# Diffusion trunk layer on one core: modulation in channel halves, q and kv in inner halves, scatter in pairs, latent tiles first

## The reference, cut to what matters

```
shift1, scale1, gate1, shift2, scale2, gate2 = split(silu(cond) @ w_ada + b_ada)
h    = x * (1 + scale1) + shift1
proj = h @ w_in        # columns: q 512 | kv 256 | k_rope 64 | hyena 3 x 1024 | gates 2 x 2048
q    = rms_norm(q_c) @ w_uq ;  kv = rms_norm(kv_c) @ w_ukv ;  attention, 8 heads
hy   = hyena(proj)     # short and long convolution
mix  = (sigmoid(g_a) * (attn @ w_o_mla) + sigmoid(g_b) * (hy @ w_o_hy)) @ w_out
x    = layer_norm(ALPHA * x + gate1 * mix)
h    = x * (1 + scale2) + shift2
aff  = softmax(h @ w_router)           # 16 experts
gate, idx = top_k(aff.T, cap)          # 16 of 128 context, 32 of 256 latent tokens an expert
ffn  = scatter_add(down(silu(gate_proj) * up_proj) * gate)
x    = layer_norm(ALPHA * x + gate2 * ffn)
```

## Time and profile before

| | us |
|---|---|
| median of 3 runs | 2348.67 (2346.88 to 2348.97) |
| profiled execution | 2348.09, span 2346.3 |
| TensorE matmul busy | 2150.9 (92%) |
| VectorE busy | 794.7 (34%) |
| ScalarE, GpSimd busy | 124.0, 54.0 |
| loads and stores | 667.79 MB, mean 285 GB/s |

### The profile page before, as it was taken

The page is one execution under the profiler, slowest core; times in us unless marked ns, Lnnn a source line. Parts: engine busy times, 40 slices in busy tenths (PEclk is TensorE's granted clock), DMA queues, the critical chain, the costliest instruction groups (busy, mean ns, idle before and its releaser), DMA issues.

```text
span 2346.3 us, 18784 instructions
## 1 busy us (share of the span) xinstructions
PE 2150.9 (92%) x8278; PEld 1069.6 (46%) x8278; DVE 794.7 (34%) x1095; ACT 124.0 (5%) x256; POOL 54.0 (2%) x99
## 2 busy tenths in 40 slices
PE   4698999999999999999999699999999999988884
PEld 1274455556555555555444363333333333332321
DVE  2201365546466658540023411112111211111116
ACT  0102310000000000000000100000000000000000
POOL 1100000000000001000100000000000000000000
PEclk9898999999999999999999899999999999999996
DMA  9943046531036666673599569999999999999992
GB/s 397 382 144 111 0 142 227 194 123 54 36 108 251 251 235 231 251 234 125 200 393 331 206 244 428 428 428 427 427 428 427 428 428 428 427 427 428 427 428 99
DMA packets 156272, 667.79 MB, mean 285 GB/s; under 512 B 9503, under 2 KB 89459, under 8 KB 116896
## 3 DMA queue, kind: packets, MB, share of 16 engines
q1 hardware_dynamic: 150544, 644.37, 69.3%
q0 software_dynamic: 5232, 19.09, 2.1%
q10 hardware_dynamic: 416, 3.15, 0.3%
HBM read 663.20 MB, written 3.38 MB: 284 GB/s over the span
## 4 chain that ended last, share of the span: by engine, by line
PE 73%; DMA 17%; DVE 9%; ACT 0%; issue 0%; ACTq 0%; DVEq 0%
PE ps L709 14%; DMA ring<-in_w_up_dram 14%; PE ps L900 10%; PE ps L866 8%; PE ps L740 7%; PE ps L1017 7%; PE ps L724 7%; DVE arena L1666 5%; PE ps L612 3%; DMA ring<-in_w_ada_dram 2%; PE ps L954 2%; PE ps L810 1%; PE ps L811 1%; PE ps L993 1%; PE ps L812 1%; PE ps L963 1%
## 5 line engine op out<-in xcount | busy, mean ns | idle before, releaser
L866 PE MATMUL ps<-ring,arena 128*64 128x512 f32 (+1 forms) x2048 | 456.3, 597 | 56.8 <-DMA ring<-in_w_up_dram 51.5
L709 PE MATMUL ps<-arena,ring 128*128 128x384 f32 x1024 | 331.9, 486 | 0.0
L866 PEld LDWEIGHTS ps<-ring,arena 128*64 128x64 f32 (+1 forms) x2048 | 142.1, 137 | 365.9 <-issue 258.9
L1239 DVE SCALAR_TENSOR_TENSOR arena<-ring,arena 128x2048 f32<-128x2048 f32 x120 | 282.2, 2352 | 54.9 <-DMA ring<-in_w_ada_dram 50.1
L709 PEld LDWEIGHTS ps<-arena,ring 128*128 128x128 f32 x1024 | 194.3, 190 | 137.5 <-issue 2.6
L900 PE MATMUL ps<-ring,arena 128*64 128x512 f32 x1024 | 227.7, 603 | 0.2
L1700 DVE TENSOR_TENSOR arena<-ps,arena 128x512 f32<-128x512 f32 x16 | 11.1, 692 | 475.5 <-PE ps L866 475.5
L740 PE MATMUL ps<-ring,arena 128*128 128x512 f32 x384 | 168.2, 598 | 3.1 <-DVE arena L1505 3.1
L724 PE MATMUL ps<-arena,ring 128*128 128x384 f32 x512 | 166.4, 486 | 0.0
L1017 PE MATMUL ps<-arena,ring 128*128 128x384 f32 x512 | 165.6, 486 | 0.0
L900 PEld LDWEIGHTS ps<-ring,arena 128*64 128x64 f32 x1024 | 73.1, 139 | 142.6 <-issue 140.6
(11 more groups left out here) (277 smaller groups left out, 1336.6 us busy)
## 6 DMA issues: line engine op xcount, KB each, us to landing
ring<-in_w_gate_dram SPq DMA_DIRECT2D x64, 2048.0 KB, 17.9
ring<-in_w_up_dram SPq DMA_DIRECT2D x64, 2048.0 KB, 18.7
ring<-in_w_down_dram SPq DMA_DIRECT2D x64, 2048.0 KB, 24.6
ring<-in_w_ada_dram SPq DMA_DIRECT2D x48, 2048.0 KB, 16.3
ring<-in_w_in_dram SPq DMA_DIRECT2D x31, 2048.0 KB, 8.5
ring<-in_w_out_dram SPq DMA_DIRECT2D x24, 2048.0 KB, 14.6
ring<-in_w_o_mla_dram SPq DMA_DIRECT2D x8, 1024.0 KB, 11.0
ring<-in_w_o_hy_dram SPq DMA_DIRECT2D x8, 1024.0 KB, 11.9
```

Of the source, the lines that this page charges most:

```text
L709: mm = pe.matmul(ps[j][:, 0:NT], w[:, k, j * P:(j + 1) * P], hT[:, k, :], start=(k == 0), stop=(k == KD - 1))
L866: mm = pe.matmul(ps[j // 4][64 * half:64 * half + m, :], xe_w[g % 2][:, c0:c0 + m], w[:, k4, half * 512:(half + 1) * 512], start=(k == 0), ...
L1239: ins = dve.scalar_tensor_tensor(sums[:, c, :], w[:, j, :], col, sums[:, c, :], ALU.mult, ALU.add)
```

## The change

1. shift1 and scale1 come in halves of the channels: eight slots hold channels 0 to 1023 of both, eight more the rest. A slot is now filled by two loads. Each half is turned to columns and modulates its eight blocks of hT by itself; the four turning matmuls read all 128 partitions of `stage`, which is set to zero first.
2. q and kv with k_rope are computed in two halves of the inner dimension. The first half of their weights goes to buffers of its own (q_half, kv_half[0]), loaded between the two halves of w_ada; its four q blocks and three kv tiles are put between the slots of w_ada and around the turning. kv and k_rope are one product of 320 columns. The sums of squares of q and the end of their norm move into and behind uq.
3. The output projection runs over the tiles in the order 1, 2, 0 (TILES); the choice among latent tokens and two of the residuals stand in column block 2 of the last tile, and the context choice is the last.
4. The scatter of the expert before is issued two matmuls at a time behind slots 1 to 6 of gate and up; on VectorE `add_outputs` stands ahead of the product that makes hid.

```diff
 
-    out = [("ada", m, k) for m in (0, 1) for k in range(8)]
-    out += [("q", 0, 0), ("q", 1, 0), ("kv", 0, 0), ("kr", 0, 0), ("uq", 0, 0), ("uq", 1, 0), ("ukv", 0, 0)]
+    out = [("ad", h, k) for h in (0, 1) for k in range(8)]
...
+        q_half = view(A_ACC, 8, QL)
+        kv_half = [view(A_MG + 2560 * h, 8, KVL + ROPE) for h in range(2)]
...
@@ -302,14 +306,19 @@
             for n, (kind, a, b) in enumerate(stream):
                 if n >= RING:
                     sp.wait_ge(used[n % RING], n // RING)
-                if kind == "ada":
+                if kind == "ad":
+                    if (a, b) == (1, 0):
+                        sp.wait_ge(S["xT_ps"], KD)
+                        sp.dma_start(q_half, w_in_v[:, 0:8, 0:QL]).then_inc(ld_wq, 16)
+                        sp.dma_start(kv_half[0], w_in_v[:, 0:8, COL_KV:COL_HY]).then_inc(ld_wkv, 16)
+                    sp.dma_start(slot(n, 2, 2, 1024)[:, 0], w_ad_v[:, 2 * b, 0:2, a * 1024:(a + 1) * 1024])\
+                        .then_inc(full[n % RING], 16)
+                    dst, src = slot(n, 2, 2, 1024)[:, 1], w_ad_v[:, 2 * b + 1, 0:2, a * 1024:(a + 1) * 1024]
+                elif kind == "ada":
                     dst, src = slot(n, 2, D), w_ada_v[:, 2 * b:2 * b + 2, a * D:(a + 1) * D]
                 elif kind == "q":
-                    dst, src = slot(n, KD, 256), w_in_v[:, :, a * 256:(a + 1) * 256]
-                elif kind == "kv":
-                    dst, src = slot(n, KD, KVL), w_in_v[:, :, COL_KV:COL_KR]
-                elif kind == "kr":
-                    dst, src = slot(n, KD, ROPE), w_in_v[:, :, COL_KR:COL_HY]
...
-            pool.dma_start(acc[:, 0, :], t["x_prompt"][0]).then_inc(ld_x2, 16)
-            pool.dma_start(gate1[:, 0, :], row(mods_dram[0, 0], P)).then_inc(ld_g1, 16)
-            pool.dma_start(acc[:, 1:3, :], t["x_sample"][0].rearrange("(a p) n -> p a n", p=P)).then_inc(ld_x2b, 16)
+            pool.dma_start(acc[:, 1:3, :], t["x_sample"][0].rearrange("(a p) n -> p a n", p=P)).then_inc(ld_x2, 16)
+            pool.dma_start(gate1[:, 1, :], row(mods_dram[0, 1], P)).then_inc(ld_g1, 16)
+            for j in range(2):
...
+            pool.memset(w_router.rearrange("p a b -> p (a b)"), 0.0).then_inc(gp, 1)
+            pool.wait_ge(gp, 2)
...
+            def q_block(h, j):
+
+                n = stream.index(("q", 1, 0))
+                w = slot(n, 8, QL) if h else q_half
+                for k in range(8):
+                    if h == 0 and j == 0:
+                        modulated_to(k)
+                    mm = pe.matmul(ps[j][:, 0:NT], w[:, k, j * P:(j + 1) * P], hT[:, 8 * h + k, :],
+                                   start=(h == 0 and k == 0), stop=(h == 1 and k == 7))
+                if h and j == 3:
+                    release(mm, n)
+                elif h:
+                    mm.then_inc(S["q_ps"], 1)
+
+            def kv_tile(h, tile):
+
+                for k in range(8):
+                    if h and tile == 0:
+                        modulated_to(8 + k)
+                    mm = pe.matmul(ps[4 + tile][:, 0:KVL + ROPE], hT[:, 8 * h + k, tile * P:(tile + 1) * P],
+                                   kv_half[h][:, k, :], start=(h == 0 and k == 0), stop=(h == 1 and k == 7))
+                if h and tile == 2:
+                    mm.then_inc(S["kv_ps"], 1)
 
             def attention(n):
...
+            for n in range(5):
                 ada(n)
             pe.wait_ge(S["sin_done"], 1)
             pe.wait_ge(S["vec_done"], 1)
             pe.matmul(ps[1][0:HID, 0:NT], fw2, fh1, start=True, stop=True).then_inc(S["filt_ps"], 1)
+            for n in range(5, 8):
                 ada(n)
+            rows_to_columns(0)
+
+            pe.wait_ge(S["xT_done"], KD)
+            pe.wait_ge(S["farg_done"], 2)
+            pe.wait_ge(ld_wq, 16)
+            q_block(0, 0)
+            q_block(0, 1)
+            ada(8)
+            q_block(0, 2)
+            q_block(0, 3)
+            ada(9)
+            ada(10)
+            pe.wait_ge(ld_wkv, 16)
+            kv_tile(0, 0)
+            for n in range(11, 16):
+                ada(n)
+            kv_tile(0, 1)
             rows_to_columns(1)
+            kv_tile(0, 2)
+            pe.wait_ge(ld_wkv2, 16)
+            for tile in range(3):
+                kv_tile(1, tile)
+            arrive(stream.index(("q", 1, 0)))
+            for j in range(4):
+                q_block(1, j)
+
             hy_n = 0
             for n in range(16, stream.index(("ga", 0, 0))):
                 kind, a, b = stream[n]
+                if kind in ("q", "ada", "x0"):
                     continue
                 arrive(n)
+                if kind == "uq":
+                    w = slot(n, 4, 768)
                     pe.wait_ge(S["q_done"], 4)
                     pe.wait_ge(S["qsq_done"], 4)
+                    if a:
                         pe.wait_ge(S["kv_tok"], 3)
+                        pe.wait_ge(S["col_done"], 2)
+                        for tile in range(3):
+                            for k in range(4):
+                                mm = pe.matmul(ps[7][:, tile:tile + 1], qsq[:, k, tile * P:(tile + 1) * P], ones,
+                                               start=(k == 0), stop=(k == 3))
+                        mm.then_inc(S["qsum_ps"], 1)
...
                         release(mm, n)
-
-                    if e:
-                        scatter(e - 1)
+                        if e and 1 <= j < 7:
+                            scatter(e - 1, 2 * j - 2, 2 * j)
 
...
-            for tile in range(3):
+            for p in range(3):
                 for cb in range(4):
-                    out_rows(tile, cb)
-                    if tile and cb == 0:
-                        h2T_copies(tile - 1)
-                    if tile == 2 and cb == 0:
-                        dve.wait_ge(S["affT_ps"], 1)
-                        link(dve.tensor_copy(taken[0:NE, 0:LC], ps[7][0:NE, 0:LC]))
-                        dve.sem_inc(S["affc_done"], 1)
-                    if tile and cb == 1:
-                        part_copy(tile - 1)
-                    if tile and cb == 2:
-                        softmax(tile - 1)
-                        residual(tile - 1)
-                spread(tile, tile + 1)
-                modulated(tile)
+                    out_rows(p, cb)
+                    if p and cb == 0:
+                        h2T_copies(p - 1)
+                    if p and cb == 1:
+                        part_copy(p - 1)
+                        softmax(p - 1)
+                    if p == 2 and cb == 2:
+                        dve.wait_ge(S["affT_ps"], 2)
+                        choose(LC, NT, 4)
+                        residual(0)
+                        residual(1)
+                spread(TILES[p], p + 1)
+                modulated(p)
             softmax(2)
+            dve.wait_ge(S["affT_ps"], 3)
             choose(0, LC, 2)
-            dve.wait_ge(S["affT_ps"], 3)
-            choose(LC, NT, 4)
...
+                if e:
+                    add_outputs(e - 1)
                 dve.wait_ge(S["sil_done"], e + 1)
                 through(dve, N_EXP + 12 * e + 7)
                 dve.tensor_tensor(hid, ps[1][:, :], sil, ALU.mult).then_inc(S["hid_done"], 1)
-                if e:
-                    add_outputs(e - 1)
```

337 lines of the change are left out of this document (157 added, 180 removed).

## The result

Before 2347.78 us (median of 4), after 2309.99 us (median of 4, 2306.3 to 2314.2): ratio 0.9839, 95% interval 0.9821 to 0.9857. A second series gave after 2308.07 us (0.9829, 0.9816 to 0.9843). The profiled run of after took 2309.47 us, its span 2307.6. The prediction was 2310.

The account below looks back on a forecast made before the run. Loads bound the front's first 94 us and the expert stage, with a serial TensorE chain between. 34.0 - 1.4 + 0.5 + 4.9 = 38.0 us off 2348.1 gives 2310, range 2300 to 2323.

Parts of the forecast that it names:

- up to uq: Kernel start to uq's first matmul: uq(0) starts at 151.3 instead of 185.25, 34.0 us earlier.
- uq to the output projection: uq onward: cold start gone gains 2.9 us, row sums lose 4.0, later rq loses 0.3; 1.4 us lost.
- output projection and routing: Latent choice moved into the last tile: 5.3 us gained, less 4.4 late out_rows and 0.4 for turning aff; 0.5 gained.
- experts and end: Last expert: down starts without the scatter ahead and follows its loads, 4.9 us gained; nothing gained in the loop.
- Loads of the front: w_ada's last slot lands at 104.9, 11.3 us later: q_half 5.4, kv_half[0] 3.6, 4 KB rows 2.3.
- That rival (2326): Front: the 1 MB issues don't run as one stream, loads 16 us beyond the estimated 2.3; 2326 us, chance 0.08.
- The cover: Front: four q_blocks and kv_tile(0,0), 25.1 us, cost nothing between w_ada slots; about 3 us in hand.
- The clock's rival: Front: TensorE's clock stays low; twenty microseconds lose 10 us of work, 3 in hand; 2317 us, chance 0.13.
- The row sums: Row sums come into the uq stage, 4.0 us lost there.
- The cold start of uq: uq's first 32 instructions took 13.45 us against 10.52 for the second; this cold start goes, 2.9 us gained.
- The 4.4 us of lateness: End of output projection: VectorE's choice, scaling and residuals take 18.4 us against TensorE's 14.0 block; last out_rows 4.4 late.
- The rival that interleaving makes TensorE the bound: Expert stage: interleaved scatter sets the pace, deciding from 1.7 us a pair; at 2.5 us a pair 2365, chance 0.03.

Follow-up runs that it names:

- blocks_behind: Against after: TensorE multiplies slots 8 to 15 of w_ada first, then the half-0 q blocks and two kv tiles, same load order; 2335.70 us.
- fill_values: Against after: 20 unused identity products on TensorE in its wait of 2.9 us ahead of the values; 2310.28 us.
- rows_8k_two: Against after: w_ada slots in rows of 8 KB, still two 1 MB issues each; modulation from wrong channels, only to time loads; 2309.32 us.
- choose_late: Against after: the choice among latent tokens alone put back behind the last softmax; tile order and residuals stay; 2313.23 us.
- scatter_whole: Against after: an expert's scatter again whole behind the last gate/up slot, VectorE's additions again behind the product making hid; 2314.18 us.

## Why the prediction was right

| step | predicted gain | measured gain |
|---|---|---|
| up to uq | 34.0 | 33.6 |
| uq to the output projection | -1.4 | -0.9 |
| output projection and routing | 0.5 | 1.6 |
| experts and end | 4.9 | 4.4 |
| sum | 38.0 | 38.6 |

The measured column is the difference of the two profiles (spans 2346.28 and 2307.65 us), each row rounded by itself.

**Loads of the front.** The last slot was forecast at 104.9 and starts at 105.0 to 105.8 in eleven profiles with 4 KB rows; the fit over the row size gave 411 GB/s at 4 KB, measured 410. The Trainium skill (DMA: Bandwidth & Descriptors, section Measured) has 341 GB/s for a load of 1 MB, issued from GpSimd. Issued from SyncE and queued one behind the other, such loads ran at 410 here and at 420 with 8 KB rows, so its figure doesn't carry over to this queue. That rival (2326) is out.

**The cover.** The mechanism was right, and blocks_behind shows it; its reserve was not: I had 3 us in hand, after had 0.44 in its profile and 0.4 to 2.9 in others. The first q_block started at 64.15 instead of 61.5. The eighth slot started at 55.23 as forecast, but its products took 3.01 us at the low clock instead of 1.90, and rows, columns and the first modulated block then took 6 us; the columns alone 1.87 at the low clock, 0.95 later. With a low clock of only a few microseconds more the blocks would have been on the path. The clock's rival was nearer than its 0.13 suggests, and that it stayed away is in part luck.

**uq to the output projection.** The row sums took 2.84, not 4.0. The cold start of uq was gone, as said, but its loss came back elsewhere, at the values (15.44 us in after, 13.90 at the full clock in fill_values). Here the sum was right through two errors of opposite sign, and by the luck of how many falls a profile has: with two to five of them the stretch varies by 4.8 us.

**Routing.** The 4.4 us of lateness came as 4.8. That the step still gained 1.6 and not 0.5 lies in the clock, a term the sum didn't have: 1.00 from 1305 to 1312 us where before had 0.50 from 1328 to 1355, so that the logits took 1.28 us where before took 1.94. rows_8k_two, the same routing at 0.50, gains only 0.3 on before; choose_late shows the same size from the other side.

**Experts.** scatter_whole gives 5.0 us for the pairs, at the last expert alone, as reasoned; the traces of before and after 4.4. The rival that interleaving makes TensorE the bound needed 1.7 us a pair; a pair costs 1.06.

## What to carry to other kernels

Where an engine waits on a stream of loads, work moved into the wait is free only up to the slack at the last load: list that slack in several profiles, since here it lay between 0.4 and 2.9 us with the same loads and the same instructions. Where the loads bound a loop, look for gains in what lets its first load start and in what follows its last, not inside. Work that is moved off a path must be added up with what already stands in the same place: the choice of 5.3 us and 10.7 us of scaling and residuals didn't fit into 14, one residual to a block did, and that was worth another 4 us.

## What the runs showed of the hardware

- The granted clock falls from 1.00 to 0.50 for about 3 us at a time, which costs about 1.5 us, in the middle of long stretches of full speed: at waits of TensorE of 2.4 to 3.1 us (2.89 at the values, 2.58 in attention, 2.44 at 601 us, 3.11 at the output projection), but also behind 24 one-column products with no wait. Not every such place shows it in every profile of the same kernel. The Trainium skill (TensorE: Matmul & The Clock Gate, section What's actually happening) says that the activity watch behind the clock runs freely and isn't reset when a kernel starts; the two profiles of after agree, with falls at 192, 278, 602 and 1117 us in the one and at 171, 195 and 280 in the other. Filling the wait at the values held the clock in that place; no run shows that the loss then moved elsewhere.
- With the scatter whole, the clock falls in the expert loop behind 11 of the 15 scatters (granted clock 0.97 over 1700 to 2000 us, 1.00 in after). It costs nothing there, since bytes are the bound; only at the last expert it costs 0.5 us.
- At a granted clock of 1.00 a product of 128 by 128 with 128 columns in f32 takes 0.232 us (20 in 4.63 us, two instructions each), a transpose of the same size 0.12 (16 in 1.91 us).
- 1 MB loads in rows of 4 KB, queued one behind the other, run at 410 GB/s, in rows of 8 KB at 420; loads of 2 MB in rows of 8 KB at 422.
